# Expert outputs as rounded two-part products with the gates applied at the slots, and a fourth pair moved behind the down products

## The reference

```python
logits = t @ router_w                          # 256 tokens x 8 experts
top_v, top_i = lax.top_k(logits, 2)
top_p = jax.nn.softmax(top_v, axis=-1)
gates = jnp.sum(jax.nn.one_hot(top_i, 8) * top_p[..., None], axis=1)
for e in range(8):
    out = out + gates[:, e:e+1] * ((silu(t @ w_gate[e]) * (t @ w_up[e])) @ w_down[e])
```

## Time and profile before

| | us |
|---|---|
| median of 3 runs | 2703.54 (2703.3 to 2706.32) |
| the profiled execution | 2704.44 |
| its span, first to last instruction | 2702.5 |
| TensorE busy | 2506.6 (93%) |
| VectorE busy | 2072.8 (77%) |
| ScalarE busy | 1257.6 (47%) |
| GpSimd busy | 271.6 (10%) |
| mean granted TensorE clock | 0.972 of full |

### The profile page before, as it was taken

One profiled execution on the slowest core, in us unless ns is written; L12 is line 12 of the kernel. 1 busy time (PEld: TensorE's weight loads), 2 busy tenths in 40 slices (PEclk: granted clock), 3 DMA queues, 4 the chain that ended last, 5 costly groups with the idle time before them and its releaser, 6 DMA issues. The chain is left out here.

```text
span 2702.5 us, 37397 instructions
## 1 busy us (share of the span) xinstructions
PE 2506.6 (93%) x14282; PEld 2161.1 (80%) x14282; DVE 2072.8 (77%) x3104; ACT 1257.6 (47%) x1540; POOL 271.6 (10%) x290
## 2 busy tenths in 40 slices
PE   5999999999999999999999999989998998778787
PEld 4789997787888888888888877747777898777786
DVE  6778984767898989899898974635748878887875
ACT  3234443236777777677777763103422333323322
POOL 0000001000000000000000000000003444333331
PEclk9999999989999999999999998999989999999999
DMA  8647675557999999999999956211558999999997
GB/s 350 245 176 285 273 286 199 216 197 286 354 356 355 356 346 344 355 353 356 353 358 354 355 190 240 114 42 67 212 236 347 412 421 420 420 421 421 421 421 298
DMA packets 109273, 824.90 MB, mean 305 GB/s; under 512 B 11864, under 2 KB 15192, under 8 KB 16096
## 3 DMA queue, kind: packets, MB, share of 16 engines
q1 hardware_dynamic: 71504, 551.75, 53.5%
q0 software_dynamic: 36864, 268.45, 24.0%
q10 hardware_dynamic: 720, 2.24, 0.2%
HBM read 821.34 MB, written 1.05 MB: 304 GB/s over the span
## 5 line engine op out<-in xcount | busy, mean ns | idle before, releaser
L1682 DVE TENSOR_TENSOR ring_r<-ring,arena_r 128x2048 fp32r<-128x2048 f32 x336 | 770.2, 2292 | 11.5
L2064 ACT ACTIVATE arena_r<-ring 128x2048 fp32r<-128x2048 f32 x378 | 725.6, 1920 | 29.0 <-DMA ring<-in_ffn_w_down 14.4
L634 PE MATMUL ps<-arena_r 128*128 128x512 f32 (+1 forms) x1120 | 417.2, 373 | 1.5 <-DVE arena_r L1718 1.5
L636 PE MATMUL ps<-arena_r 128*128 128x512 f32 x896 | 349.3, 390 | 0.0
L635 PE MATMUL ps<-ring_r,arena_r 128*128 128x512 f32 x896 | 348.6, 389 | 0.0
L1344 PE MATMUL ps<-sel,ring 128*128 128x128 f32 x2096 | 267.9, 285 | 59.7 <-ACT sel L2064 58.5
L1344 PEld LDWEIGHTS ps<-sel,ring 128*128 128x128 f32 x2096 | 251.9, 198 | 73.8 <-ACT sel L2064 71.5
L2064 ACT ACTIVATE sel<-cs,arena 128x128 f32<-128x128 f32 x256 | 102.8, 402 | 420.8 <-DVE arena L2022 381.5
L1344 PE MATMUL ps<-sel,arena 128*128 128x128 f32 x2000 | 249.5, 281 | 43.8 <-ACT sel L2064 38.1
L1344 PEld LDWEIGHTS ps<-sel,arena 128*128 128x128 f32 x2000 | 236.4, 195 | 55.3 <-ACT sel L2064 48.4
L634 PEld LDWEIGHTS ps<-arena_r 128*128 128x128 f32 x1120 | 211.3, 189 | 35.6 <-DVE arena_r L1718 1.8
(11 more groups left out here) (282 smaller groups left out, 3864.0 us busy)
## 6 DMA issues: line engine op xcount, KB each, us to landing
ring<-in_moe_w_gate SPq DMA_DIRECT2D x112, 1024.0 KB, 5.4
ring<-in_moe_w_up SPq DMA_DIRECT2D x112, 1024.0 KB, 5.5
ring<-in_moe_w_down SPq DMA_DIRECT2D x112, 1024.0 KB, 5.2
ring<-in_ada_w SPq DMA_DIRECT2D x24, 1024.0 KB, 9.6
ring<-in_ada_w SPq DMA_DIRECT2D x12, 2048.0 KB, 7.9
ring<-in_w_in SPq DMA_DIRECT2D x10, 2048.0 KB, 10.5
ring<-in_w_ada SPq DMA_DIRECT2D x8, 2048.0 KB, 10.1
ring<-in_ffn_w_gate SPq DMA_DIRECT2D x14, 1024.0 KB, 5.2
```

Source lines behind the costliest of these rows:

```text
L634: e.matmul(out, xs[0], ws[0], start=start, stop=False, skip_group_check=True)
L636: return e.matmul(out, xs[1], ws[0], start=False, stop=stop, skip_group_check=True)
L1682: v(e.tensor_tensor(ring_low[ring.half[unit]], ring.buf[unit], mo.high[unit_at[unit] % NHIGH].bitcast(F32), ALU.subtract), ("low", unit))
L2064: A.mark(e.activation(out, src, func, **kw), name)
```

## The change

What it does:

- In `route`, VectorE copies the identity and the 8 gates of each token beside each other into `m.spread` (four instructions more).
- In `prepare`, two float32 matmuls of 136 columns with `m.gath` as the weights replace the two transposes: 128 columns give slot by token, the other 8 the gates at the slots. VectorE copies the first part rounded and adds the two halves of the gate column into `m.slot_gate` (one 256-column copy as before, and two instructions of one column). The weighted one-hots (`m.scat`, two instructions per expert) go.
- ScalarE scales its copies of the result by `m.slot_gate` and writes them rounded (`m.ysbh`); VectorE makes the remainder `m.ysbl` in two new instructions, `result_low`, at the end of the iteration with `f == 0`.
- `combine` makes each output of two matmuls on rounded operands, 16 instead of 8 per expert.
- The fourth pair of `combine` moves behind the down product on TensorE; on VectorE the additions of that pair move behind the product of the activations, ahead of the low parts of the next iteration's gate weights.

```diff
@@ -367,10 +367,16 @@
             m.xgh, m.xgl = ([v4(x[i], 8) for x in xg] for i in range(2))
             m.ath, m.atl = (v4(x, 4) for x in both(512))
             m.acts = [buf(512) for _ in range(2)]
-            m.pw = [buf(256) for _ in range(2)]
-            m.scat = [buf(256).rearrange("p (t c) -> p t c", t=2) for _ in range(2)]
+            def rounded(n):
+
+                o = buf.at
+                buf(n)
+                return arena_r[:, o:o + n]
+            m.pw = [rounded(256) for _ in range(2)]
             m.gath = [buf(256).rearrange("p (t c) -> p t c", t=2) for _ in range(2)]
-            m.ysb = buf(1024)
+            m.ysbh, m.ysbl = both(1024)
+            m.slot_gate = [buf(1) for _ in range(2)]
+            m.spread = v4(buf(272), 2)
             m.lg, m.e8, m.g8, m.m8, m.oh, m.pos, m.ch = (buf(16) for _ in range(7))
             m.ix, m.fx, m.sm = buf(16).bitcast(U32), buf(16), buf(8)
             m.flag = small[:, 24:26]
@@ -967,8 +973,10 @@
                                           [(m.htm[:, t, at:at + 128], m.gath[x % 2][:, t, :]) for t in range(2)])
                         P.mark(last, ("xg", turn, x, q))
                     b = bank(("pw", turn, x), WORK)
-                    e.wait_ge(*V["onehot", turn, x])
-                    P.mark(turned(b, [m.scat[x % 2][:, t, :] for t in range(2)]), ("pw", turn, x))
+                    for t in range(2):
+                        last = e.matmul(b[:, 136 * t:136 * t + 136], m.gath[x % 2][:, t, :], m.spread[:, t, :],
+                                        start=True, stop=True)
+                    P.mark(last, ("pw", turn, x))
 
                 def split(unit):
 
@@ -1006,13 +1014,12 @@
 
                 def combine(x, pairs):
 
-                    e.wait_ge(*A["ysb", turn, x])
-                    e.wait_ge(*V["pw", turn, x])
                     for p in pairs:
+                        e.wait_ge(*V["ysb low", turn, x, p // 2])
                         b = bank(("mout", turn, x, p), WORK)
                         for j in range(2):
                             c = 128 * (2 * p + j)
-                            last = e.matmul(half(b, j), m.ysb[:, c:c + 128], m.pw[x % 2], start=True, stop=True)
+                            last = summed(half(b, j), [(y[:, c:c + 128], m.pw[x % 2]) for y in (m.ysbh, m.ysbl)])
                         P.mark(last, ("mout", turn, x, p))
 
                 prepare(0)
@@ -1024,10 +1031,10 @@
                     if f == 1 and x:
                         combine(x - 1, (0, 1, 2))
                     first("mu", i)
+                    if i:
+                        down(i - 1)
                     if f == 1 and x:
                         combine(x - 1, (3,))
-                    if i:
-                        down(i - 1)
                     b = bank(("mt", turn, i), (2,))
                     e.wait_ge(*V["mact", turn, i])
                     P.mark(turned(b, [m.acts[i % 2][:, 128 * j:128 * j + 128] for j in range(4)]), ("mt", turn, i))
@@ -1664,6 +1671,8 @@
                     v(e.tensor_scalar(tile(m.g8, t), tile(m.m8, t), m.sm[:, 4 + t:5 + t], None, ALU.mult))
                     v(e.scalar_tensor_tensor(tile(m.g8, t), tile(m.oh, t), m.sm[:, 6 + t:7 + t], tile(m.g8, t), ALU.mult,
                                              ALU.add))
+                    v(e.tensor_copy(m.spread[:, t, 0:128], ident))
+                    v(e.tensor_copy(m.spread[:, t, 128:136], tile(m.g8, t)))
                 b = taken("places")
                 v(e.scalar_tensor_tensor(m.pos, b[:, 0:16], 1.0, m.ch, ALU.add, ALU.mult))
                 v(e.tensor_scalar(m.pos, m.pos, -1.0, None, ALU.add))
@@ -1695,10 +1704,6 @@
                         at = slice(8 * t + x, 8 * t + x + 1)
                         v(e.tensor_scalar(m.gath[x % 2][:, t, :], cst("iota"), m.pos[:, at], None, ALU.is_equal),
                           ("places", turn, x))
-                    for t in range(2):
-                        at = slice(8 * t + x, 8 * t + x + 1)
-                        v(e.tensor_scalar(m.scat[x % 2][:, t, :], cst("iota"), m.pos[:, at], m.g8[:, at],
-                                          ALU.is_equal, ALU.mult), ("onehot", turn, x))
 
                 def gathered(x):
                     for q in range(2):
@@ -1707,8 +1712,22 @@
                         v(e.tensor_tensor(m.xgl[x % 2][:, c, :], v4(ps.bank["xg", turn, x, q], 4),
                                           m.xgh[x % 2][:, c, :].bitcast(F32), ALU.subtract), ("xg low", turn, x))
                         emptied(("xg", turn, x, q))
-                    v(e.tensor_copy(m.pw[x % 2], taken(("pw", turn, x))[:, 0:256]), ("pw", turn, x))
+                    b = taken(("pw", turn, x))
+                    v(e.tensor_copy(v4(m.pw[x % 2], 2), v4(b[:, 0:272], 2)[:, :, 0:128]))
+                    v(e.tensor_copy(m.slot_gate[x % 2], b[:, 128 + x:129 + x]))
+                    v(e.tensor_tensor(m.slot_gate[x % 2], m.slot_gate[x % 2], b[:, 264 + x:265 + x], ALU.add),
+                      ("pw", turn, x))
                     emptied(("pw", turn, x))
+
+                def result_low(x):
+
+                    for n in range(2):
+                        e.wait_ge(*A["ysb", turn, x, n])
+                        c = slice(512 * n, 512 * n + 512)
+                        v(e.scalar_tensor_tensor(m.ysbl[:, c], ps.bank["my", turn, x, n], m.slot_gate[x % 2],
+                                                 m.ysbh[:, c].bitcast(F32), ALU.mult, ALU.subtract),
+                          ("ysb low", turn, x, n))
+                        emptied(("my", turn, x, n))
 
                 def low(w, i, h):
                     expert_low(w, turn, i, h)
@@ -1719,8 +1738,8 @@
                       ("act low", turn, i))
                     emptied(("mt", turn, i))
 
-                def combined(x):
-                    for p in range(4):
+                def combined(x, pairs=range(4)):
+                    for p in pairs:
                         b = taken(("mout", turn, x, p))
                         for j in range(2):
                             residual(half(b, j), mod[1][:, 40:48], 2 * p + j)
@@ -1750,19 +1769,24 @@
                         low("md", i - 1, 0)
                         low("md", i - 1, 1)
                     if f == 1 and x:
-                        combined(x - 1)
+                        combined(x - 1, range(3))
                     e.wait_ge(*P["mu", turn, i, 1])
                     e.wait_ge(*A["msil", turn, i])
                     v(e.tensor_tensor(m.acts[i % 2], m.acts[i % 2], ps.bank["mu", turn, i], ALU.mult), ("mact", turn, i))
                     emptied(("mu", turn, i))
+                    if f == 1 and x:
+                        combined(x - 1, (3,))
                     if i < 55:
                         low("mg", i + 1, 0)
                         low("mg", i + 1, 1)
+                    if f == 0 and x:
+                        result_low(x - 1)
                 low("md", 55, 0)
                 low("md", 55, 1)
                 act_low(55)
                 if turn == 0:
                     over.append(e.value_load(m.over, min_val=0, max_val=1))
+                result_low(7)
                 combined(7)
 
             for l in range(2):
@@ -2253,9 +2277,10 @@
                     e.wait_ge(*P["md", turn, 7 * x + 6, 1])
                     if x:
                         e.wait_ge(*P["mout", turn, x - 1, 3])
+                    e.wait_ge(*V["pw", turn, x])
                     for n in range(2):
-                        a(m.ysb[:, 512 * n:512 * n + 512], ps.bank["my", turn, x, n], ACT.Copy, ("ysb", turn, x))
-                        emptied(("my", turn, x, n))
+                        a(m.ysbh[:, 512 * n:512 * n + 512], ps.bank["my", turn, x, n], ACT.Copy, ("ysb", turn, x, n),
+                          scale=m.slot_gate[x % 2])
 
                 gathered(0)
                 if turn:
```

## The result

The changed kernel takes 2730.64 us in the median of 6 runs (2715.81 to 2732.02), the kernel before 2703.93: a ratio of 1.0094, 95% interval 1.0078 to 1.0109. It is slower by 26.7 us between the medians (21 to 29 by the interval); 2727 was forecast, with a range of 2714 to 2733. The profiled execution took 2732.02 with a span of 2730.2, against 2704.44 and 2702.5.

The account below looks back on a forecast made before the run. TensorE was taken to bound the expert stage, with VectorE close behind. 7 x (1.85 stall + 1.3 clock + 0.25 preparation) - 0.2 = +23.6 us gave 2728.0 for the profiled execution, 2727 for the median; range 2714 to 2733.

Parts of the forecast that it names:

- The order behind the fourth pair: Gate product after each hand-over: TensorE stalls 3.45 us for VectorE's queue, net loss 1.85 us at each of seven experts.
- The new products: Expert outputs on TensorE: 16 rounded matmuls at 0.12 us each, letting the gate products begin 1.61 us earlier.
- The clock: TensorE behind each stall: granted clock falls, 1.3 us lost each, 9.1 in all; bounds 0 and 2.0 each.
- Rival A: TensorE's clock behind the stalls does not fall, or hardly: +14.5 us, 2718; chance 0.24.
- The preparation: Preparing an expert on TensorE: two float32 matmuls replace two transposes, 0.25 us more per expert, 1.8 in all.
- Covered work: VectorE's and ScalarE's other added work falls in their waits and costs nothing; uncovered, 1 us per expert.
- B: Expert stage: the wait for the fourth pair is covered, TensorE gains 9.7 us in all: 2694; chance 0.05.
- rival C: Next iteration's up and down products also wait for VectorE, 1 us more each time: 2735; chance 0.05.
- D: Two-part output products no quicker than float32, 0.20 us a matmul, about 1.2 more per expert: 2736; chance 0.03.
- The last expert: VectorE's final additions start at about 1616.1 instead of 1616.29, a gain of 0.2 us.
- The sum: Whole kernel: stall, clock and preparation over seven experts, less the last expert's gain, +23.6 us; chance 0.63.

Follow-up runs that it names:

- Low parts first: The changed kernel with VectorE making the low parts of the next gate weights ahead of the additions of the fourth pair: 2696.4 us, ratio 0.9975.
- pair put back: The changed kernel with the fourth pair back in its old place on TensorE and VectorE, rounded products and gates kept: 2697.1 us, ratio 0.9978.
- move alone: The kernel before with only the fourth pair moved on TensorE and VectorE, float32 products and gates as before: 2735.7 us, ratio 1.0118.
- late additions: The changed kernel with VectorE's additions of the fourth pair in the next iteration, behind its up and down low parts: 2688.0 us, ratio 0.9942.
- low part done twice: The kernel with late additions, with VectorE's two `result_low` instructions done twice: 2701.3 us, ratio 0.9995 to the kernel before.
- filled stall: The changed kernel with twelve useless 512-column matmuls on TensorE in front of each expert's third-iteration gate product: 2713.4 us; with four, 2721.2 us.

## Why the prediction was right, and where it was not

- **The order behind the fourth pair.** Right in mechanism and size. Predicted: a net 1.85 us from the first output product to the next gate product; measured 775.82 - 759.26 = 16.56 against 14.78, 1.78. The stall was 3.15 (3.45 was said), and VectorE waited 2.54 for the pair (2.7). Low parts first and pair put back remove it, the move alone makes it.
- **The new products.** Right: 0.12 each, and with late additions the rebuilt queue of 13.17 us is met to the hundredth, 1.61 under before. The changed kernel could not keep this, because a shorter queue on TensorE only makes it reach the stall earlier.
- **The clock.** The term that was mis-sized. Rival A (it does not fall) is excluded by the profile of after, and the fall came back at every expert. The Trainium skill tells of such a recurring fall on its page "TensorE: Matmul & The Clock Gate", section "HAM oscillation — how this bites in real kernels", and the trace agrees in that, with a low stretch behind each of seven stalls. But 7 x 1.3 = 9.1 was charged and 18.6 measured, 2.7 per stall. The single example in the earlier trace rows was a low stretch over which six matmuls ran; the first stall brought a similar one (from 777.06 to 780.47, eight matmuls), the other six one over which some thirteen ran. The bound of 2.0 was too low. The charge fits the short stretches, 1.6 us behind the first stall here (its period of 128.5 is the 128.3 that was forecast) and 1.5 in the move alone; that six of the seven would be long could not be read from one example.
- **The preparation.** Right in mechanism and size, 0.25 per expert. From the transposes ahead of the gathering to the gate product behind it the kernel before took 4.14 us (697.76 to 701.90), the changed one 4.39 (698.91 to 703.30):

```profile
697.76 0.60 PE L628 MATMUL ps<-cs,arena 128*128 128x128 f32 x4
701.90 0.47 PE L634 MATMUL ps<-arena_r,h_r 128*128 128x512 f32 x1
```
```profile
698.91 0.60 PE L634 MATMUL ps<-cs,arena 128*128 128x128 f32 x4
703.30 0.48 PE L640 MATMUL ps<-arena_r,h_r 128*128 128x512 f32 x1
```

  The terms close: 124.93 - 1.61 + 0.25 = 123.57, and the kernel with late additions has a period of 123.53.
- **Covered work.** The result's low part was hidden, as said, with 0.9 us of VectorE's wait left; the low part done twice shows that no more would have been. ScalarE's scaled copies took 1.41 us for both, where the plain ones took 1.23; that lay in its slack. Rivals B, C and D did not come: the products are fast, the stage is slower, and TensorE waits at no other place between 640 and 1630 us.
- **The last expert.** From the last down matmul to the additions 2.85 us (1646.65 to 1649.50) against 2.92: 0.1 instead of 0.2.
- **The sum.** 23.6 was forecast; the stage gave 32.1, the rest of the program gave 4.4 back, and 27.6 was left between the profiled executions. The small error of the total (3.6 us between the medians) is luck: the clock was charged 9.5 too little, the stall 1.0 too much, and the rest of the program, which was taken as unchanged, was 4.4 shorter in this execution for a reason that nothing here shows. The range also had less room than it seems: it ends at 2733, under the 2735 that rival C was given and that it was said to include. One of the six runs of the changed kernel took 2715.81 at a mean clock of 0.975 instead of 0.965 to 0.969, close to the 2713 of the filled stall; that may be an execution in which the clock mostly stayed up, but it has no trace.

## What to carry to other kernels

When work moves back in one engine's queue, look at what stands behind its consumer in the other engine's queue: the price is not only the wait but everything queued behind it that the first engine needs next. Put the consumer where its own queue has slack (here one iteration later), and the move is worth having: 2688, against 2731 as it was and 2697 with the pair put back. A recurring pause of TensorE of about 3 us may cost nearly as much again in clock as in waiting (2.7 us behind 3.15); filling it with matmuls that do nothing tells the two apart in one run.

## What the runs showed of the hardware

- The same stall of 3.15 us was followed by one of two lengths of low clock. In the changed kernel it was the short one once (eight slow 512-column matmuls, 1.6 us lost) and the long one six times (thirteen or fourteen, 2.7 to 2.9 us lost); in the move alone the short one seven times. In the long cases the clock had fallen about 0.9 us or more before the stall ended, in the short ones at most 0.4 us before its end, or after it. Nothing here shows why.
- Stalls of 2.1 us brought the clock down in three of seven cases, each time for a short stretch; seven stalls of 1.1 us (low part twice), seven of 0.6 and seven of 0.3 in none.
- The changed kernel and the move alone settle at nearly the same period (129.63 to 129.72 from the third expert on, against 129.72 to 129.83), the first with long low stretches and the second with short ones, while without the clock's fall the changed kernel has 126.87. Whether that is chance is not shown.
